# One Trainium2 core, a four-layer network in float32: the third mixer's attention by pairs of heads, and weight preparation entered at other steps

## The chip, the cores and the metric

The kernel runs on one core of one Trainium2 chip. The metric is the device time of one execution in microseconds (us), and a kernel's figure is the median of its runs. Engines are named as in the profile: PE (TensorE, its weight loads PEld), DVE (VectorE), ACT (ScalarE), POOL (GpSimd), SP (SyncE, which issues most DMAs).

## The reference

The input is 256 tokens of width 1024, with 16 meta tokens put in front (272 tokens). Everything is float32. Eight sub-layers follow each other, each as `h = h + factor * rmsnorm(f(rmsnorm(h, g)), g')`:

```python
k = 0  swiglu            k = 1  neighborhood attention (16 heads of 64)   k = 2  swiglu
k = 3  swiglu            k = 4  differential attention (8 double heads)   k = 5  swiglu
k = 6  mixer of the second block, k = 7  its MLP: square(relu(x @ w_up)) @ w_down
# k = 6, on the 256 tokens:
aq, ak, av, mq, mk, mv, mo, mi, mf = split(rms_norm(x) @ w_in)
q, k = partial_rope(aq), partial_rope(ak)        # 8 heads of 64, first 16 columns turned
att  = softmax(causal(q k^T / 8)) v              # one block of 256 keys: plain causal attention
hm   = mlstm(mq, mk, mv, mi, mf)                 # 4 heads, value width 128
hm   = hm * rsqrt(mean(hm^2) + eps) * g * sigmoid(mo)
x    = x + rms_norm(concat(att, hm) @ w_out)
```

## The kernel before, in words

**Weights.** Nearly all the time goes to products of activations with weight matrices. A product is made of three passes with rounded parts: `x_hi*w_hi + x_lo*w_hi + x_hi*w_lo` (lines 606 to 608). Weights come in panels of 1 MB or less through four slots: SP issues the DMA into `raw` (L495) once the panel three places back is used, ACT rounds it into `w_hi` (`high`, L1243), DVE forms `w_lo = raw - w_hi` (`low`, L1659), and PE waits for `w_lo`. Each sub-layer k has two phases, 2k and 2k+1; ACT, DVE and PE each walk through the panels of a phase in steps (i, j), four to a body, and every engine has an order of its own, written out by hand. Panels 0 and 1 of a phase are used together (`first_panels`, L664, L670), panel 2 goes to another bank, and panel 3 is split over two banks. Before PE may start panel 4 it waits that DVE has evacuated panels 0, 1 and 2 (`acc_free`, lines 1789 to 1791).

**Where weights are prepared.** At the end of a phase's second half (`output_steps`) ACT and DVE prepare the last panel and panels 0 and 1 of the next phase, all at the step `last - 2`. The boundary between sub-layers prepares panels 2 and 3, and panel 4 is prepared at step (0, 2) of the next phase.

**Ends of sub-layers.** Output groups are squared on ACT (L1257, the last one in halves at L1272), squares are added on POOL (L2404, L2407), and PE sums over partitions with a product with ones (`sum_most`, L839).

**Attention.** The neighborhood attention (`na_attention`) works by pairs of heads, scores L942, transposes of the probabilities L1014, products with v L1027; a small attention of the meta tokens is woven in at step 2 (scores L1153). The differential attention (`da_attention`) has scores at L959 and transposes at L1065. The third mixer (k = 6) uses `attention(k)`: 16 units, one for each of 8 heads and 2 tiles of 128 queries, with 128 or 256 keys. Per unit PE does one warm-up (a 128x128 product of ones, L855, two records), the scores (L909), one unit later the transposes (L919), two units later the products with v (L930). DVE adds the mask and takes the maximum (L1870), ACT takes the exponential (L1390), DVE copies the transposes to SBUF (L1879). Heads 2m and 2m+1 lie in one chunk m of `proj`, on partitions 0 to 63 and 64 to 127. Chunks 1 to 3 are turned by the rotary embedding at units 2, 5 and 9: PE rotates (L1120), DVE multiplies and adds (`rope_chunk`, L2074 and L2077). Before the attention DVE divides the mLSTM's result by its denominator (L2266 to L2278, semaphore `ml_norm`), which frees the banks that the rotation writes.

**Opening.** PE makes 16 warm-ups, waits for four small DMAs (`in_full`) and transposes the input.

Of the kernel before, what the change touches and what calls it, by code (L numbers as in the profile page):

```python
# [19 lines left out]
ALU = mybir.AluOpType  # L20
ACT = mybir.ActivationFunctionType
AX_X = mybir.AxisListType.X
F32 = mybir.dt.float32
# [3 lines left out]
P = 128  # L27
# [107 lines left out]
def program(nc, A, out):  # L135

    with ExitStack() as ctx:
# [69 lines left out]
        na_probs = sb("na_probs", [P, 16, NT], F32, c)  # L207
        c = [sq_at]
# [221 lines left out]
        def attention_units(k):  # L430
# [9 lines left out]
            else:  # L440
                for hd in range(8):
                    for t in range(2):
                        q = slice(64 * (hd % 2), 64 * (hd % 2) + 64)
                        w = P * (t + 1)
                        o = acc_flat[:, t, 64 * hd:64 * hd + 64]
                        units.append((proj[q, hd // 2, P * t:P * t + P], proj[q, 4 + hd // 2, 0:w], w,
                                      causal[:, NX - w:NX], 64 * hd, 64, t + 1, False, o))
# [38 lines left out]
        def _(sp):  # L486
# [117 lines left out]
        def _(pe):  # L604
# [283 lines left out]
            def attention(k, between=None):  # L888
                s = mixers[k]
                units = attention_units(k)  # L890
                n = len(units)
                for step in range(n + 2):
                    if between is not None:
                        between(step)
                    if k == NA and step in (0, 2):

                        if step == 0:
                            pe.wait_ge(s["vm_copied"], 1)
                        pe.wait_ge(s["proj"], 9 if step == 0 else 12)
                    if step == 1:  # L900
                        pe.wait_ge(s["v_copied_act"], 2)
                        if k == NA:
                            keep_warm(aux[:, 3, :], 4)
                    if step < n:
                        u = step
                        q, kk, w, bias, v0, vw, nb, rest, o = units[u]
                        wait(pe, s["logits"], u - 1)
                        keep_warm(aux[:, u % 2, 3 * P:], 1)
                        nc.tensor.matmul(aux[:, u % 2, 0:w], q, kk, start=True, stop=True).then_inc(s["scores"], 1)  # L909
                    if 1 <= step <= n:  # L910
                        u = step - 1
                        q, kk, w, bias, v0, vw, nb, rest, o = units[u]
                        pe.wait_ge(s["probs"], u + 1)
                        wait(pe, s["turned_copied"], u - 1)
                        if rest:
                            wait(pe, s["turned_rest"], u - 1)
                        bank = aux[:, 2 + u % 2, :]
                        for b in range(nb):
                            tr = nc.tensor.transpose(bank[:, P * b:P * b + P], probs[:, u % 2, P * b:P * b + P], ident[:, :])  # L919
                        if rest:  # L920
                            tr = nc.tensor.transpose(bank[0:NM, 2 * P:3 * P], probs[:, u % 2, NX:NT], ident[:, :])
                        tr.then_inc(s["turned"], 1)
                    if step >= 2:
                        u = step - 2
                        q, kk, w, bias, v0, vw, nb, rest, o = units[u]
                        pe.wait_ge(s["turned_copied"], u + 1)
                        if rest:
                            pe.wait_ge(s["turned_rest"], u + 1)
                        for b in range(nb):
                            mm = nc.tensor.matmul(o, turned[:, u % 2, P * b:P * b + P], v_rows[:, b, v0:v0 + vw],  # L930
                                                  start=b == 0, stop=b == nb - 1 and not rest)
                        if rest:
                            mm = nc.tensor.matmul(o, turned[0:NM, u % 2, 2 * P:3 * P], v_meta[:, v0:v0 + vw],
                                                  start=False, stop=True)
                        mm.then_inc(s["pv"], 1)
# [36 lines left out]
            def na_attention(between):  # L972
# [20 lines left out]
                for step in range(16 + 3):  # L993
                    if step == 1:
                        pe.wait_ge(s["v_copied_act"], 2)
                    if step == 2:
                        pe.wait_ge(s["proj"], 12)
                    between(step)
# [21 lines left out]
                    if 2 <= step <= 17:  # L1020
# [8 lines left out]
                        mm.then_inc(s["pv"], 1)  # L1029
                    if step in (10, 17):  # L1030
                        blocks_add(step // 17)

            def da_attention():
# [3 lines left out]
                for step in range(16 + 3):  # L1037
                    if step == 2:
# [56 lines left out]
            keep_warm(aux[:, 0, :], 16)  # L1095
# [26 lines left out]

            def rope_part(step):

                if step == 0:
                    pe.wait_ge(rope_done, 2)
                if step == 2:
                    pe.wait_ge(ml_norm, 4)
                if step in (2, 5, 9):
# [1372 lines left out]
```

## Time and profile before

| | |
|---|---|
| median of 3 runs | 1489.7 us (1487.86 to 1571.98; the three are 1489.7, 1571.98, 1487.86) |
| profiled execution | 1499.34 us, its span 1497.5 us, mean granted TensorE clock 0.980 |
| busy in the span | PE 1463.7 us (98%), PEld 1393.2 (93%), DVE 952.6 (64%), ACT 656.7 (44%), POOL 49.6 (3%) |
| DMA | 234 MB, mean 156 GB/s |
| chain that ended last | PE 88%, DVE 4%, DMA 2%, ACT 2%, issue 2%, POOL 1% |

A busy time is the sum of an engine's records in the span, and PE's records overlap, so 98% does not say that PE works at its peak. The chain that ended last is followed back from the last instruction, each step to what released it. A clock of 1.00 is TensorE's higher level (2.4 GHz), 0.50 its lower one (1.2 GHz).

### The profile page before, as it was taken

How to read it: one execution, taken by the hardware profiler on the slowest of the kernel's cores; microseconds unless marked ns; L12 is line 12 of the kernel's file. 1: busy time of each engine (PE TensorE's matmuls, PEld its weight loads, DVE VectorE, ACT ScalarE, POOL GpSimd, SP SyncE). 2: the span in 40 equal slices, each digit the busy share in tenths (PEclk: the TensorE clock that was granted, in tenths of full speed). 3: DMA queues.
4: the chain of work that ended last, by engine and by line, in shares of the span. 5: the costliest groups of instructions: out<-in, count | busy, mean ns of one | idle time of the engine just before them, and what ended most of it. 6: DMA issues, size and time to landing. Idle time of an engine off the chain costs nothing.

```text
span 1497.5 us, 26386 instructions
## 1 busy us (share of the span) xinstructions
PE 1463.7 (98%) x11058; PEld 1393.2 (93%) x11058; DVE 952.6 (64%) x1228; ACT 656.7 (44%) x856; POOL 49.6 (3%) x72
## 2 busy tenths in 40 slices
PE   8999999999999999999999998999999999999998
PEld 8999999968999999999999977999999987899887
DVE  6665567565865557656558575766556765787653
ACT  4443345444544335444335354543435432544432
POOL 0000010011000000000010000100001010100000
PEclk9999999999999999999999998999999996999999
DMA  6586764412455664654554510455565730346552
GB/s 211 171 225 193 204 199 150 160 31 85 143 179 184 172 206 157 198 171 151 171 185 143 171 53 29 150 189 184 171 183 157 219 113 1 113 146 204 197 177 105
DMA packets 238904, 233.99 MB, mean 156 GB/s; under 512 B 29791, under 2 KB 233492, under 8 KB 238816
## 3 DMA queue, kind: packets, MB, share of 16 engines
q1 hardware_dynamic: 237992, 232.27, 50.2%
q8 instruction: 66, 1.08, 0.3%
q10 hardware_dynamic: 824, 0.46, 0.1%
q14 instruction: 22, 0.18, 0.0%
HBM read 231.52 MB, written 1.12 MB: 155 GB/s over the span
## 4 chain that ended last, share of the span: by engine, by line
PE 88%; DVE 4%; DMA 2%; ACT 2%; issue 2%; POOL 1%; ACTq 0%; DVEq 0%; POOLq 0%; SPq 0%
PE acc L606 21%; PE acc L607 21%; PE acc L608 21%; PE acc L664 3%; PE aux L789 2%; PE aux L787 2%; PE aux L788 2%; PE aux L855 2%; PE acc L670 1%; PE aux L607 1%; PE aux L608 1%; PE aux L606 1%; PE acc L1027 1%; PE acc L1052 1%; ACT w_hi L1243 1%
## 5 line engine op out<-in xcount | busy, mean ns | idle before, releaser
L606 PE MATMUL acc<-x_hi,w_hi 128*128 128x272 f32 (+1 forms) x2008 | 575.1, 286 | 4.6 <-DVE w_lo L1659 4.4
L607 PE MATMUL acc<-x_lo,w_hi 128*128 128x272 f32 (+1 forms) x2008 | 575.2, 286 | 0.0
L608 PE MATMUL acc<-x_hi,w_lo 128*128 128x272 f32 (+1 forms) x2008 | 573.4, 286 | 0.0
L1659 DVE TENSOR_TENSOR w_lo<-raw,w_hi 128x2048 fp32r<-128x2048 f32 (+1 forms) x230 | 484.4, 2111 | 120.5 <-ACT w_hi L1243 120.0
L1243 ACT ACTIVATE w_hi<-raw 128x2048 fp32r<-128x2048 f32 (+3 forms) x251 | 406.7, 1627 | 172.1 <-DMA raw<-in_ffn_w_down 52.0
L606 PEld LDWEIGHTS acc<-x_hi,w_hi 128*128 128x128 f32 x2008 | 380.9, 190 | 7.3 <-issue 6.3
L607 PEld LDWEIGHTS acc<-x_lo,w_hi 128*128 128x128 f32 x2008 | 379.7, 189 | 0.1
L608 PEld LDWEIGHTS acc<-x_hi,w_lo 128*128 128x128 f32 x2008 | 379.7, 189 | 0.0
L606 PE MATMUL acc<-hid_hi,w_hi 128*128 128x272 f32 (+1 forms) x704 | 202.7, 288 | 0.0
L607 PE MATMUL acc<-hid_lo,w_hi 128*128 128x272 f32 (+1 forms) x704 | 201.7, 286 | 0.0
L608 PE MATMUL acc<-hid_hi,w_lo 128*128 128x272 f32 (+1 forms) x704 | 200.8, 285 | 0.0
L1789 DVE TENSOR_TENSOR z<-acc,rstd 128x544 f32<-128x544 f32 (+1 forms) x101 | 71.5, 713 | 150.6 <-PE acc L608 150.2
L1631 ACT ACTIVATE hid_hi<-z 128x544 f32 (+3 forms) x44 | 28.7, 652 | 247.7 <-DVE z L2365 247.7
L607 PEld LDWEIGHTS acc<-hid_lo,w_hi 128*128 128x128 f32 x704 | 132.6, 188 | 0.1
L608 PEld LDWEIGHTS acc<-hid_hi,w_lo 128*128 128x128 f32 x704 | 132.7, 189 | 0.0
L606 PEld LDWEIGHTS acc<-hid_hi,w_hi 128*128 128x128 f32 x704 | 132.3, 188 | 0.3
L1687 DVE TENSOR_SCALAR y<-acc,gains 128x272 f32<-128x272 f32 (+1 forms) x48 | 21.4, 487 | 59.9 <-ACT sq L1257 33.9
L664 PE MATMUL acc<-x_hi,w_hi 128*128 128x272 f32 (+1 forms) x224 | 57.8, 288 | 1.6 <-ACT x_hi L1306 1.6
L2404 POOL TENSOR_TENSOR sq_sum<-sq_sum,sq 128x544 f32<-128x544 f32 (+1 forms) x14 | 23.3, 1665 | 1037.0 <-ACT sq L1257 1006.7
L664 PE MATMUL acc<-x_hi,w_lo 128*128 128x272 f32 (+1 forms) x224 | 57.0, 285 | 0.0
L2368 DVE TENSOR_TENSOR hid_lo<-z,hid_hi 128x544 f32 (+3 forms) x44 | 31.6, 717 | 39.0 <-ACT hid_hi L1631 39.0
L855 PE MATMUL aux<-ones 128*128 128x128 f32 x308 | 50.8, 310 | 3.0 <-DVE warm L2084 1.1
(310 smaller groups left out, 1699.6 us busy)
## 6 DMA issues: line engine op xcount, KB each, us to landing
raw<-in_ffn_w_gate SPq DMA_DIRECT2D x44, 1024.0 KB, 5.3
raw<-in_ffn_w_up SPq DMA_DIRECT2D x44, 1024.0 KB, 5.3
raw<-in_ffn_w_down SPq DMA_DIRECT2D x32, 768.0 KB, 4.7
raw<-in_ffn_w_down SPq DMA_DIRECT2D x32, 640.0 KB, 4.4
raw<-in_w_up SPq DMA_DIRECT2D x16, 1024.0 KB, 5.5
raw<-in_w_down SPq DMA_DIRECT2D x16, 1024.0 KB, 4.8
raw<-in_na_w_qkv SPq DMA_DIRECT2D x12, 1024.0 KB, 5.2
raw<-in_da_w_qkv SPq DMA_DIRECT2D x12, 1024.0 KB, 5.2
```

The costliest lines, as they stand in the source:

```text
L606: nc.tensor.matmul(o, wh, xh, start=first, stop=False)
L607: nc.tensor.matmul(o, wh, xl, start=False, stop=False)
L608: return nc.tensor.matmul(o, wl, xh, start=False, stop=last)
L664: nc.tensor.matmul(banks(n, 0, j)[:, m, 0:tokens], part[:, (ph.p0 + j) % SLOTS, w], x_hi[:, k, 0:tokens], start=k == 0 and part is w_hi, s ...
L787: nc.tensor.matmul(o, mlp_hi[:, k, tok], w_hi[:, slot, w], start=first, stop=False)
L788: nc.tensor.matmul(o, mlp_hi[:, k, tok], w_lo[:, slot, w], start=False, stop=False)
L789: return nc.tensor.matmul(o, mlp_lo[:, k, tok], w_hi[:, slot, w], start=False, stop=last)
L855: nc.tensor.matmul(bank[:, 0:P], ones[:, :], ones[:, :], start=True, stop=True)
L1243: ins = nc.scalar.activation(w_hi[:, slot, w], raw[:, slot, w], ACT.Copy)
L1659: nc.vector.tensor_tensor(w_lo[:, slot, w], raw[:, slot, w], w_hi[:, slot, w].bitcast(F32), ALU.subtract)\
L1789: ins = nc.vector.tensor_tensor(dst, src, spread(0, tokens), ALU.mult)
L2368: nc.vector.tensor_tensor(hid_lo[:, dst, 0:tokens], up, hid_hi[:, dst, 0:tokens].bitcast(F32), ALU.subtract).then_inc(hid_ready, 1)
```

## The change

The third mixer's attention becomes `mix_attention` on PE, ACT and DVE. It has 8 steps instead of 16 units, with two mask operations on DVE and two exponentials on ACT a step; a step handles both heads of a chunk for one tile of queries. Each pair of scores has four warm-ups ahead of it. The rotation of chunks 1 to 3 moves to steps 1, 3 and 5, ahead of the scores on PE and behind the two mask operations on DVE. The division of the mLSTM's result (`inner_norm`) moves on DVE behind the first pair's mask operations. Its squares and their sum move to steps 5 and 6.

In the other stages: panel 1 of the next phase is prepared at the last step but one in the three mixers; panel 4 of a phase is prepared at step (0, 0) on ACT and (0, 1) on DVE, except in the first phase, where panel 3 is prepared earlier; the meta tokens' scores of the neighborhood attention move to the end of step 2; a wait of the differential attention moves from step 2 to step 3; the opening has 26 warm-ups, and the meta tokens' DMA goes first on SP's queue instead of last on ACT's.

```diff
 # PE, third mixer (attention(k, rope_part) and rope_part are removed)
+            def mix_attention():
+                s = mixers[MIX]
+                for step in range(8 + 2):
+                    if step in (1, 3, 5):
+                        m = 1 + step // 2
+                        if step == 1:
+                            pe.wait_ge(ml_norm, 4)
+                        rotate_chunk(m, acc_flat[:, 2, :])
+                        rotate_chunk(4 + m, acc_flat[:, 3, :])
+                    if step < 8:
+                        m, t = divmod(step, 2)
+                        w = P * (t + 1)
+                        pe.wait_ge(rope_done, 2 * m + 2)
+                        wait(pe, s["logits"], 2 * step)
+                        keep_warm(aux[:, 0, 3 * P:], 4)
+                        for b in range(2):
+                            q = slice(64 * b, 64 * b + 64)
+                            nc.tensor.matmul(aux[:, b, 0:w], proj[q, m, P * t:P * t + P], proj[q, 4 + m, 0:w],
+                                             start=True, stop=True).then_inc(s["scores"], 1)
+                    if 1 <= step <= 8:
+                        v = step - 1
+                        nb = v % 2 + 1
+                        pe.wait_ge(s["probs"], 2 * v + 2)
+                        wait(pe, s["turned_copied"], v - 1)
+                        for b in range(2):
+                            for kb in range(nb):
+                                tr = nc.tensor.transpose(aux[:, 2 + v % 2, P * (nb * b + kb):P * (nb * b + kb) + P],
+                                                         mix_probs[:, 2 * (v % 2) + b, P * kb:P * kb + P], ident[:, :])
+                        tr.then_inc(s["turned"], 1)
+                    if step >= 2:
+                        v = step - 2
+                        m, t = divmod(v, 2)
+                        pe.wait_ge(s["turned_copied"], v + 1)
+                        for b in range(2):
+                            hd = 2 * m + b
+                            for kb in range(t + 1):
+                                w = P * ((t + 1) * b + kb)
+                                mm = nc.tensor.matmul(acc_flat[:, t, 64 * hd:64 * hd + 64], turned_pair[:, t, w:w + P],
+                                                      v_rows[:, kb, 64 * hd:64 * hd + 64], start=kb == 0, stop=kb == t)
+                        mm.then_inc(s["pv"], 1)
 # DVE, third mixer
+            def mix_attention(inner_norm, between):
+                for step in range(8 + 1):
+                    if step < 8:
+                        m, t = divmod(step, 2)
+                        w = P * (t + 1)
+                        for b in range(2):
+                            u, col = 2 * step + b, 4 * m + 2 * b + t
+                            dve.wait_ge(s["scores"], u + 1)
+                            wait(dve, s["probs"], u - 1)
...
+                    if step == 0:
+                        inner_norm()
+                    if step in (1, 3, 5):
+                        m = 1 + step // 2
+                        rope_chunk(m, acc_flat[:, 2, :])
+                        rope_chunk(4 + m, acc_flat[:, 3, :])
+                    if step >= 1:
+                        v = step - 1
+                        w = 2 * P * (v % 2 + 1)
+                        dve.wait_ge(s["turned"], v + 1)
+                        wait(dve, s["pv"], v - 1)
+                        nc.vector.tensor_copy(turned_pair[:, v % 2, 0:w], aux[:, 2 + v % 2, 0:w])\
+                            .then_inc(s["turned_copied"], 1)
+                    between(step)
...
 # na_attention on PE: between(step) behind the scores, transposes and products of step 2
-                    if step == 2:
-                        pe.wait_ge(s["proj"], 12)
-                    between(step)
+                    if step != 2:
+                        between(step)
...
+                    if step == 2:
+                        pe.wait_ge(s["proj"], 12)
+                        between(step)
 # da_attention on PE
-                    if step == 2:
+                    if step == 3:
                         pe.wait_ge(acc_free, PHASES[2 * DA].a0 + 12)
 # opening
-            keep_warm(aux[:, 0, :], 16)
+            keep_warm(aux[:, 0, :], 26)
-            act.dma_start(meta_rows[:, :], A["meta_tokens"]).then_inc(in_full, 16)
+            sp.dma_start(meta_rows[:, :], A["meta_tokens"]).then_inc(in_full, 16)
 # output_steps on ACT (DVE: the same with low)
                     if local == last - 2 and k < MLP:
                         high(n, i, j + 3)
-                        high(n, i, j + 4)
+                        if k not in (NA, DA, MIX):
+                            high(n, i, j + 4)
+                    if local == last - 1 and k in (NA, DA, MIX):
+                        high(n, i, j + 3)
 # split on ACT: first half of a sub-layer (mixers: high(n, 0, 4) at their step (0, 0))
-                    if n == 0:
-                        high(n, i, j + 2)
                     if n == 0 and j == 0:
+                        high(n, 0, 2)
+                        high(n, 0, 3)
                         deviation_in(0, NT)
                         load_table(ACT.Silu)
+                    if n > 0 and j == 0:
+                        high(n, 0, 4)
+                    return
+                if n > 0 and isinstance(i, int) and (i, j) == (0, 2):
                     return
 # split on DVE
-                if isinstance(i, int) and i == 0 and j < 2 and n > 0:
+                if isinstance(i, int) and i == 0 and j < 3:
+                    if n == 0 and j == 0:
+                        low(n, 0, 2)
+                        low(n, 0, 3)
+                    if j == (1 if n > 0 else 2):
+                        low(n, 0, 4)
                     return
```

## Rows read from the trace of the kernel before

**Rows 1.** The page, busy time of each engine and its share of the span.
```profile
PE 1463.7 (98%) x11058; PEld 1393.2 (93%) x11058; DVE 952.6 (64%) x1228; ACT 656.7 (44%) x856; POOL 49.6 (3%) x72
```
**Rows 2.** Waits of PE: who for whom, us in total, times, longest.
```profile
PE acc L606 <- DVE w_lo L1659: 4.4, 3, 2.8
...
PE aux L839 <- POOL sq_sum L2407: 1.7, 2, 1.2
```
**Rows 3.** Windows: length, busy PE, PEld, DVE, ACT, POOL, clock, DMA.
```profile
1236.70:1240.10 3.40, 2.76 (x8) 2.18 (x9) 2.02 (x9) 0.98 (x4) 0.00 (x0) 0.50 0.00 0
...
1260.60:1264.00 3.40, 3.40 (x21) 2.38 (x21) 1.85 (x8) 1.09 (x4) 0.00 (x0) 1.00 0.00 0
```
**Rows 4.** Timeline, PE, start and last products of the third attention: start, us, engine.
```profile
1231.64 1.03 PE L1120 MATMUL aux<-proj,rotate 128*128 128x256 f32 x4
...
1234.44 0.49 PE L855 MATMUL aux<-ones 128*128 128x128 f32 x2 [0.65 <-DVE proj L2077]
...
1271.74 0.66 PE L930 MATMUL acc<-v_rows,turned 128*128 128x64 f32 x4 [0.35 <-DVE turned L1879]
```
**Rows 5.** Timeline, DVE, the division and one rotary chunk pair.
```profile
1234.30 0.16 DVE L2266 COPY stat<-acc 128x8 f32<-128x8 f32 x1
...
1235.13 1.29 DVE L2278 TENSOR_TENSOR o_rows<-acc,stat 128x512 f32<-128x512 f32 x2
...
1238.70 0.42 DVE L2074 TENSOR_TENSOR rotated<-acc,sine 128x256 f32<-128x256 f32 x1 [0.57 <-PE acc L1120]
...
1240.02 0.42 DVE L2077 TENSOR_TENSOR proj<-cosined,rotated 128x256 f32<-128x256 f32 x1
```
**Rows 6.** Timeline, PE, two units at the higher clock.
```profile
1262.99 0.44 PE L855 MATMUL aux<-ones 128*128 128x128 f32 x2
1263.36 0.70 PE L909 MATMUL aux<-proj 64*128 64x256 f32 x2
...
1264.15 0.56 PE L930 MATMUL acc<-v_rows,turned 128*128 128x64 f32 x4
...
1264.92 0.48 PE L909 MATMUL aux<-proj 64*128 64x128 f32 x2
1265.33 0.44 PE L919 MATMUL aux<-ident,probs 128*128 128x128 f32 x2
...
1265.78 0.44 PE L855 MATMUL aux<-ones 128*128 128x128 f32 x2
```
**Rows 7.** Timeline, PE, differential attention, step 2.
```profile
869.09 1.60 PE L855 MATMUL aux<-ones 128*128 128x128 f32 x12 [0.82 <-DVE proj L1791]
870.62 0.73 PE L959 MATMUL aux<-proj 64*128 64x272 f32 x4
871.28 0.44 PE L1065 MATMUL aux<-ident,da_mix 128*128 128x128 f32 x2
```
**Rows 8.** Timeline, PE, neighborhood attention, steps 2 and 3.
```profile
302.05 0.57 PE L1153 MATMUL acc<-proj 64*16 64x16 f32 x32 [1.34 <-ACT proj L1562]
302.55 0.94 PE L855 MATMUL aux<-ones 128*128 128x128 f32 x6
...
305.50 0.73 PE L942 MATMUL aux<-proj 64*128 64x272 f32 x4
```
**Rows 9.** Timeline, ACT, end of the third mixer's output.
```profile
1294.96 1.92 ACT L1243 ACTIVATE w_hi<-raw 128x2048 fp32r<-128x2048 f32 x1 [1.61 <-DMA raw<-in_w_up]
1296.79 0.58 ACT L1257 ACTIVATE sq<-acc 128x512 f32<-128x512 f32 x1
```
**Rows 10.** Timeline, DVE, first steps of the MLP.
```profile
1326.86 0.69 DVE L2344 SCALAR_TENSOR_TENSOR z<-z 128x512 f32<-128x512 f32 x1
...
1328.86 0.68 DVE L1789 TENSOR_TENSOR z<-aux,rstd 128x512 f32<-128x512 f32 x1
1330.05 2.29 DVE L1659 TENSOR_TENSOR w_lo<-raw,w_hi 128x2048 fp32r<-128x2048 f32 x1 [0.51 <-ACT w_hi L1243]
```
**Rows 11.** Timeline, DVE, first phase, panel 3's low part.
```profile
33.73 2.29 DVE L1659 TENSOR_TENSOR w_lo<-raw,w_hi 128x2048 fp32r<-128x2048 f32 x1 [1.90 <-ACT w_hi L1243]
```

More of the change, by code:

```diff
@@ L886, in turn_values @@
                     tr.then_inc(s["vm_turned"], 1)
[L888 to L893, printed above, removed]
-                        between(step)
[L895 to L921, printed above, removed]
@@ L922, in attention @@
                         tr.then_inc(s["turned"], 1)
                     if step >= 2:
[L924 to L931, printed above, removed]
@@ L1544, in step @@
                             values(k, j)
-                        if (i, j) != (2, 3) and (i, j) not in ((0, 0), (0, 1)):
+                        if (i, j) == (0, 0):
+                            high(n, 0, 4)
+                        if (i, j) != (2, 3) and (i, j) not in ((0, 0), (0, 1), (0, 2)):
                             high(n, i, j + 2)
@@ L1831, in step @@
                         low(n, i, j + 3)
-                        low(n, i, j + 4)
+                        if k not in (NA, DA, MIX):
+                            low(n, i, j + 4)
+                    if local == last - 1 and k in (NA, DA, MIX):
+                        low(n, i, j + 3)
                     if k == 0 and local in (4, 6, 9, 11):
@@ L1856, in values @@
                     .then_inc(s["v_copied"], 1)
-            def attention(k, between=None):
-                s = mixers[k]
-                units = attention_units(k)
-                n = len(units)
-                for u in range(n + 1):
-                    if between is not None:
-                        between(u)
-                    if u < n:
-                        q, kk, w, bias, v0, vw, nb, rest, o = units[u]
-                        dve.wait_ge(s["scores"], u + 1)
-                        wait(dve, s["probs"], u - 1)
-                        nc.vector.tensor_tensor_reduce(
-                            out=logits[:, u % 2, 0:w], in0=aux[:, u % 2, 0:w], in1=bias, scale=-1.0,
-                            scalar=3e38, op0=ALU.add, op1=ALU.min, accum_out=neg_max[:, u:u + 1])\
-                            .then_inc(s["logits"], 1)
-                    if u >= 1:
-                        v = u - 1
-                        nb = units[v][6]
+            def mix_attention(inner_norm, between):
+                s = mixers[MIX]
+                for step in range(8 + 1):
+                    if step < 8:
+                        m, t = divmod(step, 2)
+                        w = P * (t + 1)
+                        for b in range(2):
+                            u, col = 2 * step + b, 4 * m + 2 * b + t
+                            dve.wait_ge(s["scores"], u + 1)
+                            wait(dve, s["probs"], u - 1)
+                            nc.vector.tensor_tensor_reduce(
+                                out=logits[:, b, 0:w], in0=aux[:, b, 0:w], in1=causal[:, NX - w:NX], scale=-1.0,
+                                scalar=3e38, op0=ALU.add, op1=ALU.min, accum_out=neg_max[:, col:col + 1])\
+                                .then_inc(s["logits"], 1)
+                    if step == 0:
[7 more added lines that the diff above has]
+                        w = 2 * P * (v % 2 + 1)
@@ L2292, in between_units, with between @@
+                        squares = sq[:, :, :, :].rearrange("p a b n -> p (a b n)")[:, 0:D]
+                        def between(step):
+                            if step == 5:
                                 for t in range(2):
```

107 lines of the change are left out of this document (34 added, 73 removed).

## Prediction

> **What bounds the kernel now.** I read the page first, then the waits of PE, then windows with the clock, then the timeline around each place that the change touches. PE is busy in 98% of the span, the next engine in 64% [rows 1], and in the chain of waits it holds 88%. So a part of the change counts only where PE stands idle, runs at the lower clock, or gets more or less work. Idle PE is small: the waits for `w_lo` are 4.4 us in three places, those for the sum of squares on POOL 1.7 us in two [rows 2]. The one large place is the third mixer's attention, from the first warm-up at 1234.44 to the last products at 1271.74 plus 0.5, which is 37.8 us [rows 4]. PE falls to the lower level before its window at 1236.7 and is back at the higher one in the window at 1260.6 [rows 3]: 23.9 us at 0.50. Ahead of the fall PE had waited in two pieces, one of them from 1233.8 to 1234.44 for the rotary result.
>
> **The third attention, at the higher clock.** The old unit pair takes 2.79 us, from 1262.99 to 1265.78 [rows 6], and PE is never late for another engine there; 16 units would be 22.3 us, and with three rotations, the late start and the tail I make it 29.2 us for the whole stretch: 37.8 less 8.6 us, which the low clock cost if 17.2 of the 23.9 us were PE's own work and would halve (the rest is PE waiting for weights to load or for its order).
>
> The new step is worked out from these durations. One warm-up is 0.37 us [rows 6], twelve records are 1.53 us [rows 7], so four warm-ups (eight records, 0.11 us each more) are 1.04 us. A pair of scores on the two halves of the partitions runs together: 0.66 us for four records 272 wide [rows 7], while one alone is 0.63 us at 256 and 0.41 us at 128 [rows 6]; I take 0.63 and 0.42 for a pair. Transposes are 0.28 us for two [rows 6], so 0.5 for four; products are 0.40 us for four [rows 6], so 0.45 and 0.9 for four and eight with their start. A pair of rotations is about 0.95 us [rows 4]. On DVE the division is 2.12 us, 1234.30 to 1236.42, and a rotary chunk pair 1.74 us, 1238.70 to 1240.44 [rows 5]. Two mask operations of 256 wide and the way to them I take at 1.0 us.
>
> The order now does harm. The division sits behind the first pair's masks, and PE's first rotation waits for it. Step 0: warm-ups and scores until 1235.9; masks until 1236.5; division until 1238.7: PE idle 2.8 us. Step 1: rotation, warm-ups, scores, transposes, until 1241.6. Step 2 needs the turned chunk, which DVE makes behind its masks: 1241.35 + 1.0 + 1.74, so PE waits until 1244.1, idle 2.5 us, then works 2.4 us. Step 3 is 3.8 us of work (until 1250.2), step 4 waits until 1251.8 and works until 1254.2, step 5 works until 1258.0, step 6 waits 1.6 us and works until 1261.9, step 7 until 1264.7; the last transposes wait for the exponentials until 1265.8, and the last products end near 1267.6. That is **33.1 us at the higher clock, 3.9 us more than the old order would take**. Half of the scores' time and none of the warm-ups' is saved, and 8.5 us of waits at steps 1, 2, 4 and 6 take what is saved.
>
> **The clock.** In the old order the fall cost 8.6 us. In the new one PE has 2.8 and 2.5 us of idleness within the first 8 us, more than ahead of the old fall, so I expect a fall at the start here too. How long it stays is open. Bounds: none (33.1 us), or the whole stretch. At the lower level a record takes twice its time: warm-ups 0.9 us more a step, scores 0.3 to 0.5, products 0.4 to 0.9, while DVE's waits stay; for eight steps and three rotations that is some 14 us, so 47 us. The old fall is the nearest row: the clock stayed low for 23.9 us though PE was called busy all along [rows 3]. But a pair of heads now gets eight warm-ups where it had four, so I take half of that length, 12 to 13 us, nearly all PE's own work: 6.5 us. That makes 39.6 us against 37.8: **+1.8 us**.
>
> The Trainium skill ("TensorE: Matmul & The Clock Gate", Part 1: The HAM clock gate) has it that the low level is the default, and that sustained matmul activity releases it. By that rule the eight groups of warm-ups would end each fall early, and the attention would come near 33.1 us plus a short fall, some 35 us; that is the first rival below.
>
> **The other edits**, each against the same profiled execution:
> - First phase. PE starts panel 3 at 36.08, as `w_lo`, made from 33.73 to 36.02, is ready [rows 11]; the panel ahead ended 0.7 us before. Both parts of that panel are now made ahead of the deviation, while its raw data had landed long before: **-0.7**. The opening itself: the meta tokens' DMA comes earlier, but 26 warm-ups last until about 8.5 and PE's first transposes were at 8.74: -0.1, bounds 0.5 to both sides.
> - Neighborhood attention. PE waits 1.34 us for the last projection at 302.05 [rows 8]. Now warm-ups (0.87), scores (0.65), transposes (0.5) and products (0.93) come first, from about 300.6 (302.05 less the wait) to 303.55, and then the meta scores (0.5) until 304.05. But DVE's next masks stand behind the meta scores: the sums (0.47), a mask, a reduction and a mask bring PE's next scores to 305.9 instead of 305.50 [rows 8]. So the wait moves and nothing is won: **+0.4**, bounds -1.3 and +0.6.
> - Differential attention. PE waited 0.82 us on the evacuation before the warm-ups at 869.09 [rows 7]; scores and masks need nothing of it, and their followers (the mix, the transposes at 871.28) were ready before: **-0.9**.
> - Outputs of the mixers. In the third, ACT's `w_hi` of panel 1 waits 1.61 us for its DMA and ends only as the square starts at 1296.79 [rows 9], though its products were done at 1294.8; POOL ends late and PE waits 1.2 us of the 1.7 [rows 2]. With the square first, both waits go: **-1.9** for the two mixers (1.3 and 0.6 with the weight load). The panel made later has 5 us until it is used.
> - Panel 4 prepared earlier. Of 4.4 us in three places [rows 2] the MLP has 2.8: `w_lo` at 1330.05 to 1332.34 is too late [rows 10]. But PE also needs panel 2's evacuation (1328.86). On DVE `low` now goes ahead of the square at 1326.86 [rows 10]; it takes 2.2 us, then 2.0 us of that step follow, and the evacuation ends at 1331.7. PE starts at 1331.9 instead of 1332.48: **-0.6**, and in the fifth FFN, in the same way, -0.2. What is late next is the evacuation. The other first halves lose nothing: their panel 4 comes 2 to 4 us later than its evacuation would.
>
> Sum: -0.7 - 0.1 + 0.4 - 0.9 - 1.9 - 0.8 = -4.0; with +1.8 it is **-2.2 us**. Against the profiled 1499.3 us that gives 1497.1. The median of the runs shown is 1489.7, 9.6 us lower; with the same difference the forecast is **1487.5 us**, no change that a measurement can tell: about 2% (30 us) is what can be told from none here.
>
> **Rivals.**
> 1. The clock holds, or comes back within 4 us. For it: twice the warm-ups per pair. Against it: the idle pieces of 2.8 and 2.5 us, and the 23.9 low us with a busy PE [rows 3]. Attention 33.1 + 1.9 = 35 us, so -2.8 - 4.0 = -6.8: 1483. Chance 0.22. The rule quoted above from the Trainium skill's page speaks for this one.
> 2. Slower than before: the clock stays low. The place is the run of waits at steps 1 to 6, the price that of 16 more warm-ups at 0.21 us a record on PE's own path. It decides once the low stretch passes 17 us (8.7 us of cost: 41.8 - 37.8 = 4.0, what the other edits save); at its full length 47 - 37.8 - 4.0 = +5: 1495. If the runs at 1489.7 had no fall in this attention at all (their 9.6 us is close to the 8.6), the new falls come on top: +1.8 + 8.6 - 4.0 = +6.4: 1496. Chance 0.30 for both together.
> 3. The earlier `low` delays evacuations in more phases than I counted, or the edits outside do not do what they say: then the 4.0 us shrink to 1 or less and the time is 1490 to 1491. Chance 0.08.
>
> My forecast has the remaining 0.40. The range that holds 8 in 10 goes from 1480 to 1498, with the run-to-run spread of the two close runs of before (1.8 us). Faster by over 2% needs 30 us, and all idle PE and all low clock at the places touched do not come to that: 0.02. Slower by over 2%: 0.02.
>
> **What would show it.** In the changed profile: PE idle 2 to 3 us ahead of the first rotation, and its releaser the division's result; further waits on `rope_chunk` at steps 2, 4 and 6; the attention 35 to 43 us long; the two waits at L839 of the mixers and that at panel 3 gone; the MLP's wait still about 2 us, but for DVE's evacuation. I would be wrong if PE's waits in the attention were under 3 us in sum, or if windows there stayed at 1.00 throughout.

## The result, and the profile after

The changed kernel takes **1497.6 us** (median of seven runs, 1490.7 to 1504.3) against 1487.9 us for the kernel before in the same sessions: a ratio of **1.006, 95% interval 1.0035 to 1.0085**. The median of 1487.9 us has one slow run of 1572.0 us in it, which the ratio leaves out. A gain of 2 us was forecast; the kernel is slower by 5 to 13 us. The profiled execution of the changed kernel has a span of 1499.8 us, only 2.3 us more than the 1497.5 us of the one before. That one was a long run of its kernel: 95 further runs have a mean of 1489.7 us, and it lies 9.6 us above.

The page after, busy time of each engine; [rows 1] is its counterpart. PE has 52 more instructions, and no engine has become a new bound.

```profile
PE 1469.2 (98%) x11110; PEld 1400.0 (93%) x11110; DVE 951.1 (63%) x1220; ACT 655.7 (44%) x856; POOL 50.4 (3%) x72
```

The waits of PE after (who for whom, us in total, times, longest):

```profile
PE aux L850 <- DVE proj L2069: 4.9, 4, 2.1
PE acc L1110 <- DVE o_rows L2273: 2.6, 1, 2.6
PE acc L601 <- DVE z L1772: 2.6, 2, 2.1
...
PE aux L930 <- DVE neg_max L1879: 1.6, 1, 1.6
```

The waits for `w_lo` and `sq_sum` of [rows 2] are gone. In their place PE waits 7.5 us in the third attention (the first two rows; `L850` are the warm-ups, `L1110` the rotation), 2.6 us for evacuations, and 1.6 us ahead of scores of the neighborhood attention. That last row is the one that matters. Timeline of PE there (start, us, engine line, tiles, count, idle before and its releaser), to be held against [rows 8]:

```profile
301.11 1.00 PE L1014 MATMUL acc<-v_rows,turned_pair 128*128 128x64 f32 x8
302.04 0.57 PE L1129 MATMUL acc<-proj 64*16 64x16 f32 x32
304.23 1.23 PE L930 MATMUL aux<-proj 64*128 64x272 f32 x4 [1.62 <-DVE neg_max L1879]
```

The wait of 1.34 us for the projection is gone, and one of 1.62 us stands behind the meta scores. Windows of the same stretch (window, length, busy PE, PEld, DVE, ACT, POOL, clock, DMA share, GB/s), the first of the changed kernel, then one of the kernel before:

```profile
300.90:304.30 3.40, 1.78 (x46) 1.61 (x44) 1.64 (x8) 0.70 (x3) 0.04 (x1) 1.00 0.77 262
304.30:307.70 3.40, 3.40 (x16) 2.70 (x16) 2.32 (x7) 1.64 (x6) 0.84 (x4) 0.50 0.05 7
...
324.80:328.20 3.40, 3.40 (x8) 0.66 (x5) 0.00 (x0) 0.00 (x0) 0.00 (x0) 0.50 0.00 0
328.20:331.60 3.40, 3.40 (x29) 2.69 (x27) 3.11 (x10) 1.24 (x5) 0.40 (x2) 1.00 0.00 0
```

```profile
304.30:328.20 23.90, 22.95 (x158) 16.20 (x157) 15.77 (x55) 10.72 (x37) 3.62 (x18) 1.00 0.04 10
```

PE was idle for half of the window up to 304.3; then its clock is at the lower level for 23.9 us, where the kernel before stays at the higher one. The two traces can be set against each other at the issue of each weight panel's DMA, which comes when an earlier panel is used. So read, the changed kernel gains 1.3 us by 42 us, loses 8.8 us in the neighborhood attention, gains 8.6 us in pieces, and loses 3.4 us in the third mixer up to the end of its attention.

Two of these differences have a part that belongs to the one execution of the kernel before. In the stretch of the 8.8 us it had 6.8 us at 0.50 of its own (from 345.8 on), so the loss is understated. And some 3 us of the 8.6 us lie between 614 and 787 us, where it waited 3.0 us for ACT once; e7, a version without any edit there, waits 0.4 us. The row of the kernel before (waits of PE: us in total, times, longest):

```profile
PE aux L839 <- ACT sq L1272: 4.3, 2, 3.0
```

The third attention shows the gaps that were forecast, and two shorter falls in place of the long one of [rows 3]. Windows of the changed kernel: the stage of gated heads ahead of it, whose code is unchanged, the attention's first 9.1 us, its fall, and the rest.

```profile
1225.90:1229.30 3.40, 3.40 (x12) 2.53 (x11) 1.74 (x4) 0.80 (x2) 1.29 (x2) 0.50 0.00 0
...
1240.68:1249.80 9.12, 4.60 (x30) 3.50 (x30) 4.56 (x18) 1.97 (x8) 0.00 (x0) 1.00 0.00 0
1249.80:1256.60 6.80, 6.59 (x26) 5.79 (x27) 1.69 (x7) 0.88 (x4) 0.00 (x0) 0.50 0.00 0
1256.60:1275.80 19.20, 15.89 (x123) 13.40 (x122) 11.81 (x37) 7.06 (x23) 0.00 (x0) 1.00 0.00 1
```

Its timeline of PE, with the pieces of idleness; it answers to [rows 4]:

```profile
1240.68 1.16 PE L850 MATMUL aux<-ones 128*128 128x128 f32 x8 [0.31 <-DVE proj L2069]
1241.77 0.49 PE L901 MATMUL aux<-proj 64*128 64x128 f32 x4
1244.90 1.13 PE L1110 MATMUL acc<-proj,rotate 128*128 128x256 f32 x4 [2.64 <-DVE o_rows L2273]
...
1250.01 2.07 PE L850 MATMUL aux<-ones 128*128 128x128 f32 x8 [2.09 <-DVE proj L2069]
...
1260.56 1.16 PE L850 MATMUL aux<-ones 128*128 128x128 f32 x8 [1.24 <-DVE proj L2069]
...
1268.01 1.16 PE L850 MATMUL aux<-ones 128*128 128x128 f32 x8 [1.24 <-DVE proj L2069]
...
1276.17 1.00 PE L850 MATMUL aux<-ones 128*128 128x128 f32 x7
```

From the first warm-up to the next stage it is 35.5 us, where the trace before has 37.8.

### The profile page after: what moved, and what is told of

The parts are those of the page before. It is cut to its first block, busy times and chain, and to the rows that moved or that the text cites. A ratio compares the mean times of both kernels' runs of the same rounds, so it can differ in the third digit from the quotient of the medians.

```text
span 1499.8 us, 26467 instructions
## 1 busy us (share of the span) xinstructions
PE 1469.2 (98%) x11110; PEld 1400.0 (93%) x11110; DVE 951.1 (63%) x1220; ACT 655.7 (44%) x856; POOL 50.4 (3%) x72
## 4 chain that ended last, share of the span: by engine, by line
PE 90%; DVE 4%; ACT 2%; issue 2%; DMA 1%; POOL 0%; POOLq 0%; DVEq 0%; SPq 0%
PE acc L602 21%; PE acc L601 21%; PE acc L603 21%; PE acc L659 3%; PE aux L850 2%; PE aux L784 2%; PE aux L782 2%; PE aux L783 2%; PE acc L665 1%; PE aux L602 1%; PE aux L603 1%; PE aux L601 1%; PE acc L1014 1%; PE aux L930 1%; PE aux L1001 1%
## 5 line engine op out<-in xcount | busy, mean ns | idle before, releaser
L850 PE MATMUL aux<-ones 128*128 128x128 f32 x360 | 52.3, 295 | 6.4 <-DVE proj L2069 4.9
L850 PEld LDWEIGHTS aux<-ones 128*128 128x128 f32 x360 | 48.8, 209 | 8.5 <-DVE proj L2069 5.6
```

The costliest lines, as they stand in the source:

```text
L850: nc.tensor.matmul(bank[:, 0:P], ones[:, :], ones[:, :], start=True, stop=True)
```

## The experiments

**How they are read.** Runs of one kernel differ by up to 18 us, so every run's granted clock was used. (1 - mean clock) x 2 x span is its time at the lower level, called low time here: 69 us for the changed kernel's profiled run, whose stretches at 0.50 sum to 71. Over all 225 runs that list a clock, with one constant per kernel and one slope, the time is that constant plus **0.375 us per low us**, with a scatter of 0.8 us. The constant is an estimate of the time with no low clock, the kernel's work and its waits, as far as that mean price holds for the place where the clock was low; the neighborhood attention will show a higher one. The table has each kernel's mean time, mean low time with its standard error, the constant, and the ratio to the kernel before with its 95% interval. The ratio is taken against runs of the same sessions, so it differs a little from that of the means.

| kernel (runs) | mean us | low us | no low time | ratio |
|---|---|---|---|---|
| before (95) | 1489.7 | 38.1 +-1.0 | 1475.4 | |
| changed (7) | 1497.7 | 57.3 +-4.4 | 1476.2 | 1.006 [1.0035, 1.0085] |
| e1 third attention alone (12) | 1492.1 | 34.3 +-2.8 | 1479.2 | 1.0008 [0.9982, 1.0033] |
| e2 all but the third attention (12) | 1491.4 | 52.4 +-3.9 | 1471.8 | 0.9993 [0.997, 1.0016] |
| e3 neighborhood wait put back (12) | 1489.2 | 37.7 +-1.8 | 1475.1 | 0.9986 [0.9964, 1.0008] |
| e4 DVE order in third attention (12) | 1489.9 | 55.8 +-1.2 | 1469.0 | 0.9995 [0.9976, 1.0014] |
| e5 hole filled, six warm-ups (12) | 1488.3 | 37.9 +-1.7 | 1474.1 | 0.9995 [0.9977, 1.0014] |
| e6 e3 and e4 (8) | 1480.3 | 32.9 +-2.0 | 1468.0 | 0.9939 [0.9918, 0.996] |
| e7 neighborhood edit alone (12) | 1495.0 | 50.3 +-3.8 | 1476.2 | 1.0046 [1.0021, 1.007] |
| e8 e6, one warm-up per pair (6) | 1478.1 | 35.4 +-3.3 | 1464.8 | 0.9923 [0.9896, 0.9951] |
| e9 edits outside both (12) | 1483.5 | 33.1 +-2.7 | 1471.1 | 0.9956 [0.9934, 0.9977] |
| e10 e8, hole filled instead (6) | 1475.2 | 28.5 +-3.6 | 1464.5 | 0.9897 [0.9871, 0.9923] |
| e11 e8, gated heads warmed (7) | 1478.1 | 30.8 +-4.6 | 1466.5 | 0.9918 [0.9889, 0.9948] |
| e12 hole filled, two warm-ups (12) | 1488.9 | 37.2 +-1.8 | 1475.0 | 0.9993 [0.9972, 1.0014] |

**The neighborhood edit alone, and put back (e7, e3).** e7 is the kernel before with this; e3 is the changed kernel without it:

```
                 for step in range(16 + 3):
-                    if step == 2:
-                        pe.wait_ge(s["proj"], 12)
-                    between(step)
+                    if step != 2:
+                        between(step)
...
+                    if step == 2:
+                        pe.wait_ge(s["proj"], 12)
+                        between(step)
```

> The kernel before with the neighborhood attention's edit alone (the wait for the last projection and the meta scores behind the products of step 2). Theory A: +0.4 to +1.0 us of work, and 15 to 20 us more at the lower clock in each run, from a fall near 305: +6 to +8 us against the kernel before. If the fall needs the other edits too (the earlier phases shift what stands there), within 2 us of the kernel before. The forecast put this edit at +0.4 us, with bounds of -1.3 and +0.6.

> The changed kernel with one part undone: the wait for the last projection of the neighborhood attention and its meta scores stand at the start of step 2 again, as before. Theory A: the 1.8 us of idle PE at 302.4 become the old 1.3 us, the clock stays at the higher level until about 345, and the time is 7 to 9 us under the changed kernel, so within 1 us of the kernel before. Theory B: at most 1 us under the changed kernel, +7 to +9 us against the kernel before. A third: the clock falls in the neighborhood attention by chance, whatever stands there; then this trace shows a fall near 304 too.

e7 is 5.3 us over the kernel before (3 to 10 us by the interval of its ratio), with 12.2 low us more. Its windows show the cause as the changed kernel does, at the same place:

```profile
301.90:305.30 3.40, 1.78 (x46) 1.61 (x43) 1.67 (x8) 0.72 (x3) 0.07 (x1) 1.00 0.82 275
305.40:329.30 23.90, 23.90 (x90) 16.03 (x88) 9.02 (x31) 6.52 (x23) 2.28 (x12) 0.50 0.01 2
329.30:332.70 3.40, 3.40 (x30) 2.80 (x28) 3.22 (x10) 1.35 (x5) 0.39 (x2) 1.00 0.00 0
```

e3 is 8.5 us under the changed kernel, with 19.6 low us fewer. Its trace has the old wait of 1.35 us at 301.18, and no stretch below 1.00 between 19 and 899 us. All four traces with the moved wait and nothing in its hole (changed, e2, e4, e7) have a fall at 304 to 306, of 20.5 to 23.9 us; none of the others has one there. Two more pairs of the table differ in this edit alone: e2 is 7.9 us over e9, with 19.3 low us more, and e4 is 9.6 us over e6, with 22.9. In all four pairs a low us more goes with 0.41 to 0.43 us.

The panels' DMAs separate the clock from the work. Timeline of SP, the last DMA ahead of the fall and the next one, in the changed kernel, then in e3 (old order), then in e5 (changed order with the hole filled, see below):

```profile
298.95 0.37 SPq L489 DMA_DIRECT2D raw<-in_na_w_o  x1
363.44 0.39 SPq L489 DMA_DIRECT2D raw<-in_ffn_w_gate  x1
```

```profile
299.43 0.37 SPq L489 DMA_DIRECT2D raw<-in_na_w_o  x1
352.24 0.39 SPq L489 DMA_DIRECT2D raw<-in_ffn_w_gate  x1
```

```profile
300.18 0.37 SPq L489 DMA_DIRECT2D raw<-in_na_w_o  x1
353.07 0.39 SPq L489 DMA_DIRECT2D raw<-in_ffn_w_gate  x1
```

That is 64.5 us against 52.8 and 52.9. All nine traces with no low clock in this stretch have 52.8 or 52.9 us, in the old order and in the changed one with its hole filled. The changed kernel and e7 have 27.3 low us in it (the fall and a short one near 356) and take 64.5 us, e2 23.9 and 62.9, e4 20.5 and 61.4, the kernel before 6.8 and 55.7: 0.42 to 0.43 us for each low us. So the moved work costs some 0.1 us, and the rest is the clock. The constants of e7 and of the changed kernel stand 0.8 and 1.1 us above their partners' mostly because they price these low us at 0.375: 0.05 us more on 12.2 and 19.6 low us is 0.6 and 1.0.

The fall isn't in every execution. One run of e7 has 27 low us in all, which leaves no room for one of 23.9 beside the 15 us or more that every run shows, while the twelve of e4 have 51 to 63.

**The hole filled (e5, e12).** The changed kernel with work that nobody needs in the hole:

```
                         pe.wait_ge(s["proj"], 12)
                         between(step)
+                        keep_warm(aux[:, 2, :], 6)
```

> The changed kernel with six warm-ups (twelve records, 1.5 us by [rows 7]) behind the meta scores of the neighborhood attention, where its trace shows PE idle for 1.8 us; nothing else differs, and the scores behind them wait for the masks as before. If it is the idle piece that sends the clock down (theory A, first form): the stretch from 304 on stays at the higher level, the low time of a run falls from a mean of 57 us to about 38, and the time by 7 us at a cost of 0 to 0.3 us of PE's own work. If the fall comes from the order of the work there, whatever fills the hole (second form), the fall near 304 stays and the time is that of the changed kernel within 1 us.

Timeline of PE in e5, and below it a window of e5:

```profile
303.27 0.57 PE L1130 MATMUL acc<-proj 64*16 64x16 f32 x32
303.77 1.60 PE L850 MATMUL aux<-ones 128*128 128x128 f32 x12
305.47 0.73 PE L930 MATMUL aux<-proj 64*128 64x272 f32 x4
```

```profile
304.30:328.20 23.90, 22.86 (x156) 15.99 (x155) 15.82 (x56) 10.71 (x37) 3.63 (x18) 1.00 0.03 6
```

Work was added and the kernel is 9.4 us faster than the changed one; low time fell from 57 to 38 us. So the changed order doesn't bring the fall by itself: with its hole filled, the fall isn't there. e12 has two warm-ups there:

> The changed kernel with two warm-ups behind the meta scores of the neighborhood attention, where six held the clock: of the 1.8 us hole about 1.3 us stay open, as long as the wait that the kernel before has two microseconds earlier. If the clock answers to the length of the one idle piece, it holds as in the kernel before: low time near 38 us, 1488 us. If PE must be kept at work over the whole stretch of short products and waits, the fall near 304 comes in some or all runs: low time 45 to 58 us and 1491 to 1497 us.

```profile
303.22 0.71 PE L850 MATMUL aux<-ones 128*128 128x128 f32 x4
304.91 0.73 PE L930 MATMUL aux<-proj 64*128 64x272 f32 x4 [0.98 <-DVE neg_max L1880]
```

With 0.98 us of idleness left, where the changed kernel has 1.62, low time is 37 us and the clock of that stretch stays at 1.00. These are two sizes at one place; what decides between them isn't settled.

**The other two parts apart (e1, e2, e9).** e1 is the kernel before with `mix_attention` on the three engines (and its buffer); e2 is the changed kernel with the old `attention` and division; e9 has, on the kernel before, only edits like these:

```
-                if isinstance(i, int) and i == 0 and j < 2 and n > 0:
+                if isinstance(i, int) and i == 0 and j < 3:
...
-                    if step == 2:
+                    if step == 3:
                         pe.wait_ge(acc_free, PHASES[2 * DA].a0 + 12)
...
-            keep_warm(aux[:, 0, :], 16)
+            keep_warm(aux[:, 0, :], 26)
```

> The kernel before with the third mixer's new attention alone (pairs of heads, four warm-ups ahead of each pair's scores, the division and the turned chunks behind the masks); every other edit is left out. Theory A (the loss is in the neighborhood attention, where the changed kernel's trace has 1.8 us of idle PE ahead of the scores and 23.9 us at the lower clock that the trace before does not have): this kernel stays within 2 us of the kernel before, 0 to +2 us. Theory B (the loss is this attention: its waits at the higher clock make it 33 us where the old order takes 29, and the extra warm-ups do not keep the clock up): +4 to +8 us against the kernel before. In both, four waits of PE of 2.8, 2.3, 1.5 and 1.5 us at the steps 1, 2, 4 and 6.

> The changed kernel with the third mixer's attention and its division put back as they were before; all other edits stay. Theory A (the moved wait of the neighborhood attention costs about 8.8 us through the clock, the other edits save 4 to 6): +3 to +5 us against the kernel before, and the clock in the neighborhood attention is low from about 304 on, for 20 us or more. Theory B (the third attention is the loss): -3 to -5 us against the kernel before. If the two effects add and the changed kernel's +9 us is their sum with the -4 of the rest, this one has +4 and the kernel with the third attention alone has +4 to +5.

> The kernel before with the edits outside the two attentions alone: opening and first phase, differential attention, outputs of the mixers, panel 4. The forecast put them at -0.7 - 0.1 - 0.9 - 1.9 - 0.8 = -4.4 us. If the sum of terms was right and no clock answers to them: with no low time 1471 us (1475.5 for the kernel before), a low time of about 38 us as before, and so -4 to -5 us against the kernel before. If they cost clock as the neighborhood edit does, their low time is over 45 us and the time within 2 us of the kernel before.

With no low time the new attention costs **+3.8 us** (1479.2 - 1475.4), and the edits outside give **-4.3 us** (1471.1 - 1475.4). The sum is -0.5, and e3, which has both and the old neighborhood order, has -0.3: the work adds up. Low time doesn't: e1 has 4 us less than the kernel before, e9 5 less, e7 12 more, so 3 more in sum, where the changed kernel has 19 more. With a standard error of 3 to 4 us on each of these, e2 still fits (7 expected, 14 found) and the changed kernel does so poorly. That a fall comes in more of the runs of one version than of another would do this; what decides it isn't tested.

Of the two theories in the expectations, A had the place of the larger loss right, and B the added work of the new attention (33 us where the old order takes 29), but not the 4 to 8 us that B gave e1: it is +2.4 us in the mean, and its interval includes no change. Theory A's sizes for e2 missed: 1.7 us over the kernel before in place of 3 to 5.

e2 and e7 also show the old attention outside the one trace of [rows 3]. In e7, timeline of PE, its first warm-up and its last products, and a window from the one to the other:

```profile
1237.94 0.49 PE L855 MATMUL aux<-ones 128*128 128x128 f32 x2 [0.65 <-DVE proj L2079]
...
1266.90 0.66 PE L930 MATMUL acc<-v_rows,turned 128*128 128x64 f32 x4 [0.35 <-DVE turned L1881]
```

```profile
1237.94:1267.30 29.36, 27.03 (x148) 20.16 (x148) 19.52 (x69) 10.02 (x34) 0.00 (x0) 0.94 0.00 1
```

It takes 29.5 us, with 3.4 us of it at 0.50. The 23.9 low us of [rows 3] belonged to that execution, not to the order: e2 and e9 have 13.7 low us in the gated heads and none in this attention.

**DVE's order in the third attention (e4, e6).** The changed kernel, with on DVE:

```
                 for step in range(8 + 1):
+                    if step == 0:
+                        inner_norm()
+                    if step in (1, 3, 5):
+                        m = 1 + step // 2
+                        rope_chunk(m, acc_flat[:, 2, :])
+                        rope_chunk(4 + m, acc_flat[:, 3, :])
                     if step < 8:
...
-                    if step == 0:
-                        inner_norm()
-                    if step in (1, 3, 5):
...
```

> The changed kernel with DVE's order changed in the third attention: the division stands ahead of the first pair's masks, and the turned chunk of steps 1, 3 and 5 ahead of that step's masks. The neighborhood attention keeps its moved wait. PE's waits of 2.8, 2.3, 1.5 and 1.5 us there (8.1 us in sum) should shrink to 2 us or less in sum, and the attention from 35.4 us to 28 to 30 us. Theory B: -5 to -8 us against the changed kernel, as far as the clock stays up, more if its falls in that stage go too. Theory A: the same -5 us or so, but +3 us or more against the kernel before remain, with the lower clock from 304 to 328. If the waits only go elsewhere (PE waiting for masks at the odd steps), the gain is under 2 us.

> The changed kernel with both repairs: the neighborhood attention's wait at the start of step 2 as in the kernel before, and in the third attention the division and the turned chunks ahead of the masks. If the two effects stand apart and add: with no low time 1475.9 - 1.0 - 7.2 = 1467.7 us (from the regression over the runs so far: 1475.9 changed, 1474.9 with the first repair, 1468.7 with the second), and with 38 us of low time at 0.38 us each 1482, which is 8 us under the kernel before. If the clock takes back what the order gives (the denser attention brings more falls), 1486 or more.

e4 has 7.2 us less work and waits than the changed kernel, with the same low time, so 7.8 us less in the mean; still it is no faster than the kernel before. (The expectation had it 3 us or more slower.) With the neighborhood wait put back as well (e6) the gain stays: 9.4 us under the kernel before. Timeline of PE in e6, the first steps and the end:

```profile
1229.06 1.16 PE L850 MATMUL aux<-ones 128*128 128x128 f32 x8 [0.57 <-DVE proj L2067]
1230.15 0.49 PE L901 MATMUL aux<-proj 64*128 64x128 f32 x4
1231.10 1.13 PE L1108 MATMUL acc<-proj,rotate 128*128 128x256 f32 x4 [0.46 <-DVE o_rows L2271]
...
1234.71 1.13 PE L850 MATMUL aux<-ones 128*128 128x128 f32 x8 [0.59 <-DVE neg_max L1859]
...
1254.99 1.38 PE L850 MATMUL aux<-ones 128*128 128x128 f32 x5
```

The idle pieces of 2.64, 2.09, 1.24 and 1.24 us are now 0.46, 0.59, none and none, and the attention takes 25.9 us.

**The warm-ups (e8, e11), and the best version (e10).** One warm-up for four ahead of each pair's scores on e6; three for one in the gated heads on e8; and on e8 the changed order of the neighborhood attention with six warm-ups behind it, as in e5:

```
-                        keep_warm(aux[:, 0, 3 * P:], 4)
+                        keep_warm(aux[:, 0, 3 * P:], 1)
...
-                            keep_warm(acc_flat[:, 2 + step // 2, :], 1)
+                            keep_warm(acc_flat[:, 2 + step // 2, :], 3)
```

> The kernel with both repairs, and one warm-up ahead of each pair's scores in the third attention where there were four. Of 24 warm-ups (48 records at 0.13 us, 6.2 us) 4 to 6 us lie on PE's own path, less what then is waited for on DVE and ACT. If the warm-ups did nothing for the clock: low time as in the kernel with both repairs, and 3 to 5 us less time. If they hold the clock up: the attention falls for 15 us or more longer at the lower level, and the time is the same or up to 3 us more.

> The kernel with both repairs and one warm-up per pair, with three warm-ups where there was one in each of the first four steps of the stage ahead of the third attention (its gated heads), whose traces all show 13.7 us at the lower clock from about 1214 on. Eight more warm-ups are 2.1 us of PE's work. If they only lie in the low stretch and do not shorten it: +1 to +3 us. If they hold the clock or end the fall 7 us or more earlier: 0 to -2 us, and low time down by 7 to 13 us a run.

> The kernel with both repairs and one warm-up per pair, but with the neighborhood attention in the changed order and its hole filled by six warm-ups, in place of the old order. By the runs with no low time the filled form is 1.1 us shorter than the old order (1474.2 against 1475.3), with the same low time: 1464 with no low time, 1477 as it runs, 1 us under the kernel with the old order. If the warm-ups only hold the clock by chance there, low time is over 50 us in part of the runs and the time 1480 or more.

e8: 3.2 us less with no low time and 2.5 +-3.9 low us more. The three extra warm-ups cost their time and their use can't be seen. e11: 1.7 us more work, and 4.6 +-5.6 low us fewer, worth as much; its trace has no low time in the gated heads (up to 1226.4), where that of e8 has 13.7 us, but its mean time is that of e8. A draw. Windows of e11, the heads, then a fall of 3.4 us in its attention:

```profile
1212.00:1226.40 14.40, 13.77 (x85) 10.85 (x84) 6.51 (x19) 3.20 (x8) 5.13 (x8) 1.00 0.21 73
1228.90:1232.30 3.40, 3.40 (x12) 1.95 (x10) 2.17 (x7) 0.73 (x5) 0.00 (x0) 0.50 0.00 0
```

e10 is the fastest of all, 1475.2 us in the mean, ratio 0.9897 [0.9871, 0.9923], 14.5 us under the kernel before; against e8 its 0.3 us of work and 7 +-5 low us are not surely a gain.

## Why the prediction was wrong

The sum of the forecast was -2.2 us; measured in the mean was +8.0 us (1497.7 - 1489.7). By its steps:

**The neighborhood term failed: +0.4 us, with bounds of -1.3 and +0.6.** Its wait was foreseen: DVE's next masks stand behind the meta scores, and so the wait moves. At the higher clock, with the hole filled, the moved work was measured at 0.1 us (52.9 us against 52.8). What the step left out is what an idle PE does to its clock there. It priced the hole as a wait alone, though the same text took two idle pieces for the reason to expect a fall in the third attention. The moved hole is 1.62 us against 1.34 [rows 8], right behind short products; then 20 to 24 us run at the lower level. In the traces that is 8.6 to 11.7 us (the latter with the short fall near 356); in the means, where not every run has the fall, +5.3 us (e7) to +9.6 us (e4 against e6), where the upper bound was +0.6. Of the 10.2 us between forecast and measurement this term holds 4.9 (e7) to 8.1 (e3 against the changed kernel), and the rest isn't assigned. The bounds came from the nearest waits, and none of them could hold a cost that comes after the wait is over.

**The third attention was right in its work, and its size came out near by luck: two errors in the clock offset each other.** 33.1 us against 29.2 us at the higher clock, +3.9 us, was the forecast; +3.8 us was measured. The gaps of 2.8, 2.5, 1.6 and 1.6 us were measured at 2.64, 2.09, 1.24 and 1.24, and the first has the releaser that was named. The old order's 29.2 us is e7's 29.5. The new order was to have a fall of 12 to 13 us and take 39.6 us; the changed trace has 6.8 low us in it and 35.5 us. And the fall that it was set against is not the old order's: the 8.6 us that the old attention was to lose are there in one trace of four (the kernel before, e2, e7, e9). In the mean, new against old is +2.4 us (e1), for a forecast of +1.8.

**The edits outside were right in their sum: -4.4 us forecast, -4.3 us measured.** They weren't run apart; the waits that the trace names are these. PE's 0.5 us for `w_lo` at panel 3 of the first phase is gone, and so are the 1.7 us for POOL's sums of [rows 2]. In the trace the third mixer's output has the square ahead of `w_hi`, and no wait for the DMA, which answers to [rows 9] (timeline of ACT):

```profile
1298.70 0.60 ACT L1233 ACTIVATE sq<-acc 128x512 f32<-128x512 f32 x1 [1.41 <-PE acc L603]
1299.20 1.90 ACT L1219 ACTIVATE w_hi<-raw 128x2048 fp32r<-128x2048 f32 x1
```

In the MLP `w_lo` goes first and the evacuation is late, as foreseen; it answers to [rows 10] (DVE, then PE):

```profile
1329.74 2.29 DVE L1637 TENSOR_TENSOR w_lo<-raw,w_hi 128x2048 fp32r<-128x2048 f32 x1
...
1333.93 0.68 DVE L1772 TENSOR_TENSOR z<-aux,rstd 128x512 f32<-128x512 f32 x1
...
1334.67 0.39 PE L601 MATMUL acc<-x_hi,w_hi 128*128 128x256 f32 x1 [2.12 <-DVE z L1772]
```

The wait is 2.12 us where that for `w_lo` was up to 2.8 [rows 2]. In the differential attention the 0.82 us ahead of the warm-ups [rows 7] are gone (`871.98`, no wait).

**The rivals.** Rival 1 (the clock holds in the third attention, or comes back within 4 us) was nearer there than the forecast: it gave the attention 35 us, and 35.5 was measured. Rival 2 had the sign and nearly the size, 1495 or 1496, but put the fall in the wrong stage. Rival 3 is refuted by e9.

**The base.** The forecast moved the profile's difference onto the median. That is sound only if a profiled run's low time is typical: 61.5 us of stretches at 0.50 in the one before, against a mean of 38 in 95 runs; (61.5 - 38) x 0.375 is 8.8 of its 9.6 us of excess.

The Trainium skill ("TensorE: Matmul & The Clock Gate", Part 1: The HAM clock gate) says that the low level is the default and that sustained matmul activity releases it. e5 agrees: with work in the hole, the clock stays up. By the same sentence the fall near 304 would have ended early, as PE was called busy throughout; in e7 it lasted 23.9 us with 23.90 us of busy PE, so busy records alone didn't release it here.

## What to carry to other kernels

Price an idle piece of PE twice, as the wait and as the clock that may fall behind it (here 0.1 us, and 5 to 10 us in the mean), and before a wait is moved ask what fills the new hole; a few matmuls that nobody reads were cheaper than the hole. On an engine that serves the bound one, work that the bound engine waits for goes ahead of work for the next step: e4's order gave 7.2 us with no instruction added or removed. Where runs of one kernel differ by more than the change can do, fit their times against their low times and compare work and clock apart.

## What the runs showed of the hardware

- A microsecond at the lower clock cost 0.375 us in the mean of 225 runs, and 0.42 to 0.43 us in the neighborhood attention (five traces with low clock there against nine without), where the ratio of the two levels alone would give 0.5. Why it is less isn't shown.
- A fall may last long with PE at work: 23.9 us at 0.50 after a hole of 1.62 us, while the kernel before has a hole of 1.34 us two microseconds earlier and no fall behind it.
- The low time of the kernel before ranged from 18 to 60 us, and 42 x 0.375 = 16 us is most of its spread of 18.5 us (1480.4 to 1498.9).
- Low times of the parts did not add (3 us in sum, 19 in the changed kernel), while their work did (-0.5 us in sum, -0.3 in e3). Whether that is more than the scatter of seven runs isn't settled.
